# Reordering a gated-linear-attention output stage by tile shape, and its gate matmul as two row tiles

## The reference, cut to what matters

```python
gate_logit = (glr @ p['gla_w_gate_up'] + p['gla_b_gate'])      # rank 16 -> 128 per head
log_a = log_sigmoid(gate_logit) / GLA_TAU
bcum = cumsum(log_a within a chunk)
q_t, k_t, k_end = qc * exp(bcum), kc * exp(-bcum), kc * exp(b_last - bcum)
A = where(causal, q_t @ k_t^T, 0)
o_intra = A @ vc
dS = k_end^T @ vc
S_next = exp(b_last) * S + dS
o_inter = q_t @ S_start
o = rms_norm(o_intra + o_inter) * silu(gog)
```

## Time and profile before

| | before |
|---|---|
| median of 3 runs | 1530.92 us |
| lowest, highest | 1530.88, 1531.73 us |
| the profiled execution's own time | 1532.95 us |
| its span | 1531.2 us |
| granted TensorE clock, mean | 0.998 |
| PE matmul busy | 98% of the span |
| DVE, ACT busy | 45%, 40% |

### The profile page before, as it was taken

The page is one execution under the profiler, slowest core; times in us unless marked ns, Lnnn a source line. Parts: engine busy times, 40 slices in busy tenths (PEclk is TensorE's granted clock), DMA queues, the critical chain, the costliest instruction groups (busy, mean ns, idle before and its releaser), DMA issues.

```text
span 1531.2 us, 25468 instructions
## 1 busy us (share of the span) xinstructions
PE 1499.9 (98%) x9798; PEld 1393.1 (91%) x9798; DVE 691.3 (45%) x1190; ACT 606.9 (40%) x1100; POOL 10.8 (1%) x25
## 2 busy tenths in 40 slices
PE   6999999999999999999999999999999999999998
PEld 6989999999999999998988989998998998998986
DVE  5555555542358774233544453245432323323335
ACT  5333333322147772134554642134541441531532
POOL 1000000000000000000000000000100000000000
PEclk9999999999999999999999999999999999999999
DMA  5556445432312222232432422253122222222222
GB/s 160 151 133 163 126 125 156 108 86 70 82 50 80 74 69 73 83 100 56 115 106 63 113 82 73 76 186 97 42 74 77 71 81 83 69 82 68 78 89 82
DMA packets 224962, 143.58 MB, mean 94 GB/s; under 512 B 7655, under 2 KB 211112, under 8 KB 224893
## 3 DMA queue, kind: packets, MB, share of 16 engines
q1 hardware_dynamic: 224900, 142.72, 32.8%
HBM read 129.86 MB, written 12.84 MB: 93 GB/s over the span
## 4 chain that ended last, share of the span: by engine, by line
PE 85%; DVE 6%; ACT 4%; issue 3%; DMA 1%; SPq 1%; DVEq 0%; ACTq 0%
PE psum L591 55%; PE psum L1007 18%; PE psum L748 1%; PE psum L776 1%; DMA w_raw<-in_w_in_dram 1%; PE psum L639 1%; PE psum L931 1%; DVE arena L1938 1%; ACT arena L1392 1%; PE psum L602 1%; DVE arena L1994 1%; PE psum L759 1%; PE psum L974 1%; PE psum L972 1%; PE psum L708 1%
## 5 line engine op out<-in xcount | busy, mean ns | idle before, releaser
L591 PE MATMUL psum<-XH,w_hi 128*128 128x320 f32 x1872 | 589.9, 315 | 3.8 <-ACT arena L1382 1.8
L591 PE MATMUL psum<-XH,w_lo 128*128 128x320 f32 x1872 | 579.7, 310 | 0.0
L591 PE MATMUL psum<-XL,w_hi 128*128 128x320 f32 x1872 | 579.6, 310 | 0.0
L1662 DVE TENSOR_TENSOR w_lo<-w_raw,w_hi 128x1024 fp32r<-128x1024 f32 x177 | 216.5, 1223 | 355.4 <-ACT w_hi L1194 354.7
L591 PEld LDWEIGHTS psum<-XH,w_hi 128*128 128x128 f32 x1872 | 352.3, 188 | 16.9 <-issue 8.9
L591 PEld LDWEIGHTS psum<-XL,w_hi 128*128 128x128 f32 x1872 | 352.4, 188 | 0.7
L591 PEld LDWEIGHTS psum<-XH,w_lo 128*128 128x128 f32 x1872 | 352.0, 188 | 0.0
L1194 ACT CAST w_hi<-w_raw 128x1024 fp32r<-128x1024 f32 x177 | 185.2, 1047 | 306.3 <-PE psum L1007 154.1
L1007 PE MATMUL psum<-w_hi,YL 128*128 128x512 f32 x280 | 109.1, 390 | 0.0
L1007 PE MATMUL psum<-w_hi,YH 128*128 128x512 f32 x280 | 109.1, 390 | 0.0
L1007 PE MATMUL psum<-w_lo,YH 128*128 128x512 f32 x280 | 109.1, 390 | 0.0
(11 more groups left out here) (276 smaller groups left out, 1713.8 us busy)
## 6 DMA issues: line engine op xcount, KB each, us to landing
w_raw<-in_w_in_dram SPq DMA_DIRECT2D x88, 512.0 KB, 3.9
w_raw<-in_w_up_dram SPq DMA_DIRECT2D x32, 512.0 KB, 4.1
w_raw<-in_w_down_dram SPq DMA_DIRECT2D x32, 512.0 KB, 3.5
w_raw<-in_w_branch_dram SPq DMA_DIRECT2D x24, 512.0 KB, 3.8
arena<-in_cache_fox_k_dram SPq DMA_DIRECT2D x8, 1024.0 KB, 5.8
arena<-in_cache_fox_v_dram SPq DMA_DIRECT2D x8, 1024.0 KB, 7.9
out_dram<-arena SPq DMA_DIRECT2D x16, 256.0 KB, 2.4
arena<-in_state_gla_dram SPq DMA_DIRECT2D x4, 1024.0 KB, 5.6
```

The costliest lines, as they stand in the source:

```text
L591: mm = pe.matmul(Z[h][:, 0:HT], w[s][:, k, :], x[:, k, h * HT:(h + 1) * HT], start=(k == 0 and i == 0), stop=(k == KT - 1 and i == 2))
L1662: dve.tensor_tensor(dst, src, h.bitcast(F32), ALU.subtract).then_inc(w_lo, 1)
```

## The change

The outputs get a bank each, GO = banks 6, 7, 4, 5, 2, and PE does first all five full matmuls, then the eight 64-column ones, then the eight 32-column ones; go_done is signalled as each tile's last matmul ends. The waits for go_read between outputs go; one wait for all five readouts now stands before the sample states, since they reuse banks 2, 4 and 5. The turned outputs go to banks 6, 7 and 4 (O_TURN), and only the last tile's two transposes wait for a state signal, the seventh, which frees bank 4. The gate's input glr is laid out as two tiles of token halves, one in rows 0 to 15 and one in rows 32 to 47, GU is loaded twice, and each gate matmul uses its own 32-row tile of the array; gu_in then counts 32 a head.

```diff
--- before.py
+++ after.py
@@ -156,6 +156,7 @@
             return ctx.enter_context(nc.semaphore(name))
 
 
+        GRP = 2 * TS_
         psum = ctx.enter_context(nc.psum_tensor("psum", [P, 8, 512], F32))
         bank = [psum[:, i, :] for i in range(8)]
         Z = bank[0:2]
@@ -183,7 +184,7 @@
         col = sb("col", [P, KT, NR])
         lru_c4 = sb("lru_c4", [P, 2, LRU_N])
         bcol = sb("b_fox_col", [FOX_HEADS, 1])
-        glr = sb("glr", [GLA_RANK, T])
+        glr = sb("glr", [2 * GRP, HT])
         cn = sb("c_nat", [P, NT, FOX_HEADS])
         small = sb("small", [P, 12, 8])
         lfn = sb("logf_nat", [P, NT, FOX_HEADS])
@@ -313,7 +314,6 @@
 
             return v[:, TP:T].rearrange("p (b t) -> p b t", t=TS_)
 
-        GRP = 2 * TS_
         NGRP = NB // 2
 
         def parted(v):
@@ -326,6 +326,12 @@
 
         def grp(g):
             return slice(g * GRP, (g + 1) * GRP)
+
+        def rank_rows(q):
+            return slice(q * GRP, q * GRP + GLA_RANK)
+
+        GO = [bank[i] for i in (6, 7, 4, 5, 2)]
+        O_TURN = [bank[i] for i in (6, 7, 4)]
 
         def tok(t):
             return slice(t * P, (t + 1) * P)
@@ -509,7 +515,8 @@
                 if not first:
                     load(b, s, w_in_v[:, :, c(cgk, P)])
                     sp.wait_ge(gg_mm, h.v)
-                sp.dma_start(GU[0:GLA_RANK, :], gla_up[0][:, c(0, P)]).then_inc(gu_in, 16)
+                for q in range(2):
+                    sp.dma_start(GU[rank_rows(q), :], gla_up[0][:, c(0, P)]).then_inc(gu_in, 16)
                 load(b + 1, 1 - s, w_in_v[:, :, c(cgv, GLA_DV)])
                 load(b + 2, s, w_in_v[:, :, c(cgv, GLA_DV, P)])
                 if not first:
@@ -878,10 +885,11 @@
             def turn_o(h):
 
                 pe.wait_ge(go_ready, (h + 1).v)
-                pe.wait_ge(ds_read, (h * 8 + 8).v)
                 for t in range(NT):
+                    if t == NT - 1:
+                        pe.wait_ge(ds_read, (h * 8 + 7).v)
                     for e in range(2):
-                        mm = pe.transpose(TBK[t // 2][:, (2 * (t % 2) + e) * P:(2 * (t % 2) + e + 1) * P],
+                        mm = pe.transpose(O_TURN[t // 2][:, (2 * (t % 2) + e) * P:(2 * (t % 2) + e + 1) * P],
                                           OS[:, t, e * P:(e + 1) * P], idf[:, :])
                 mm.then_inc(gt_turned, 1)
 
@@ -894,14 +902,14 @@
 
                     if some:
                         turn_o(h + -1)
-                    pe.wait_ge(gu_in, (h * 16 + 16).v)
+                    pe.wait_ge(gu_in, (h * 32 + 32).v)
                     if some:
                         pe.wait_ge(ds_read, (h * 8).v)
                         pe.wait_ge(at_ready, (h * 2).v)
                     else:
                         pe.wait_ge(last_sb, 1)
                     for q in range(2):
-                        mm = pe.matmul(SBK[q][:, 0:HT], GU[0:GLA_RANK, :], glr[:, q * HT:(q + 1) * HT], start=True, stop=True)
+                        mm = pe.matmul(SBK[q][:, 0:HT], GU[rank_rows(q), :], glr[rank_rows(q), :], start=True, stop=True)
                     mm.then_inc(gg_mm, 1)
 
                 def turn_ke():
@@ -945,6 +953,7 @@
                         rows = grp(i // 2)
                         return KEM[rows, i % 2, :], VN[rows, NTP, :]
                     pe.wait_ge(kem_ready, (h + 1).v)
+                    pe.wait_ge(go_read, (h * 5 + 5).v)
                     pe.wait_ge(ds_read, (h * 8 + 4).v)
                     pe.wait_ge(at_ready, (h * 2 + 2).v)
                     states(DS_SAMPLE, part)
@@ -960,30 +969,24 @@
                         if t >= 3:
                             mm.then_inc(at_done, 1)
 
-                def out(t):
-
-                    O = (TBK[2], OBK)[t % 2]
-                    if t == NTP:
-                        pe.wait_ge(s0_in, (h * 16 + 16).v)
-                    pe.wait_ge(at_ready, (h * 2 + (1 if t < NTP else 2)).v)
-                    if t >= 2:
-                        pe.wait_ge(go_read, (h * 5 + (t - 1)).v)
-                    if t < NTP:
-                        pe.matmul(O[:, 0:GLA_DV], AT[:, t, :], VN[:, t, :], start=True, stop=False)
+                def out_tiles():
+
+                    for t in range(NT):
+                        if t in (0, NTP):
+                            pe.wait_ge(at_ready, (h * 2 + (1 if t < NTP else 2)).v)
+                        pe.matmul(GO[t][:, 0:GLA_DV], AT[:, t, :], VN[:, t, :], start=True, stop=False)
+                    for t in range(NTP):
                         for c in range(2):
-                            mm = pe.matmul(O[c * GLA_CH:(c + 1) * GLA_CH, 0:GLA_DV], QG[:, t * P + c * GLA_CH:t * P + (c + 1) * GLA_CH],
-                                           SA[:, 2 * t + c, :], start=False, stop=True)
-                    else:
-                        pe.matmul(O[:, 0:GLA_DV], AT[:, t, :], VN[:, t, :], start=True, stop=False)
-                        for c in range(2):
-                            for g in range(NGRP):
-                                mm = pe.matmul(O[grp(g), 0:GLA_DV], QGB[:, c, grp(g)], S0[:, 2 * g + c, :], start=False,
-                                               stop=(c == 1))
+                            mm = pe.matmul(GO[t][c * GLA_CH:(c + 1) * GLA_CH, 0:GLA_DV],
+                                           QG[:, t * P + c * GLA_CH:t * P + (c + 1) * GLA_CH], SA[:, 2 * t + c, :],
+                                           start=False, stop=True)
+                        mm.then_inc(go_done, 1)
+                    pe.wait_ge(s0_in, (h * 16 + 16).v)
+                    for c in range(2):
+                        for g in range(NGRP):
+                            mm = pe.matmul(GO[NTP][grp(g), 0:GLA_DV], QGB[:, c, grp(g)], S0[:, 2 * g + c, :], start=False,
+                                           stop=(c == 1))
                     mm.then_inc(go_done, 1)
-
-                def out_tiles():
-                    for t in range(NT):
-                        out(t)
 
                 block(b, s, XH, XL, (gate, None))
                 block(b + 1, 1 - s, XH, XL)
@@ -1228,7 +1231,7 @@
 
                 act.wait_ge(z_done[h], 1)
                 step(act.activation(fz[0:FOX_HEADS, h * HT:(h + 1) * HT], Z[h][0:FOX_HEADS, 0:HT], ACT.Identity, bias=bcol[:, :]))
-                act.copy(glr[:, h * HT:(h + 1) * HT], Z[h][32:32 + GLA_RANK, 0:HT]).then_inc(z_free[h], 1)
+                act.copy(glr[rank_rows(h), :], Z[h][32:32 + GLA_RANK, 0:HT]).then_inc(z_free[h], 1)
 
             def first_q(h, O):
 
@@ -1446,7 +1449,7 @@
                 for j in range(3):
                     n = 2 if j < 2 else 1
                     for e in range(2):
-                        src = TBK[j].rearrange("p (t e d) -> p t e d", e=2, d=P)[:, 0:n, e, :]
+                        src = O_TURN[j].rearrange("p (t e d) -> p t e d", e=2, d=P)[:, 0:n, e, :]
                         dst = OT[:, e, 2 * j * P:(2 * j + n) * P].rearrange("p (t d) -> p t d", d=P)
                         ins_ = act.activation(dst, src, ACT.Copy, scale=col[:, e, R_GN:R_GN + 1])
                     ins_.then_inc(gt_copied, 1)
@@ -1519,7 +1522,7 @@
                         act.activation(half(SG[:, e, :], q), Z[q][:, 0:HT], ACT.Tanh, scale=0.5).then_inc(sg_tanh, 1)
                         if (e, q) == (1, 0):
                             for t in range(NT):
-                                O = (TBK[2], OBK)[t % 2]
+                                O = GO[t]
                                 act.wait_ge(go_done, (h * 5 + (t + 1)).v)
                                 step(act.copy(OS[:, t, :], O[:, 0:GLA_DV]))
                                 act.activation(E2[:, 0:GLA_DV], O[:, 0:GLA_DV], ACT.Square,
```

More of the change, by code:

```diff
@@ L961, in scores @@
                             mm.then_inc(at_done, 1)
-                def out(t):
-                    O = (TBK[2], OBK)[t % 2]
-                    if t == NTP:
-                        pe.wait_ge(s0_in, (h * 16 + 16).v)
-                    pe.wait_ge(at_ready, (h * 2 + (1 if t < NTP else 2)).v)
-                    if t >= 2:
-                        pe.wait_ge(go_read, (h * 5 + (t - 1)).v)
-                    if t < NTP:
-                        pe.matmul(O[:, 0:GLA_DV], AT[:, t, :], VN[:, t, :], start=True, stop=False)
-                        for c in range(2):
-                            mm = pe.matmul(O[c * GLA_CH:(c + 1) * GLA_CH, 0:GLA_DV], QG[:, t * P + c * GLA_CH:t * P + (c + 1) * GLA_CH],
-                                           SA[:, 2 * t + c, :], start=False, stop=True)
-                    else:
-                        pe.matmul(O[:, 0:GLA_DV], AT[:, t, :], VN[:, t, :], start=True, stop=False)
-                        for c in range(2):
-                            for g in range(NGRP):
-                                mm = pe.matmul(O[grp(g), 0:GLA_DV], QGB[:, c, grp(g)], S0[:, 2 * g + c, :], start=False,
-                                               stop=(c == 1))
-                    mm.then_inc(go_done, 1)
```

## The result

The changed kernel takes 1521.53 us, median of 6 runs (1520.51 to 1522.85), against 1530.83 of the kernel before (6 runs too): ratio 0.9941, 95% interval [0.9931, 0.9951], 9.3 us less, by the interval 7.5 to 10.6.

What follows compares the result with a forecast made beforehand. The prediction took TensorE, busy 98% of the span, as the bound. It summed 0.53 (head 0's gate) + 5.04 (three head-to-head stretches) + 1.61 (after head 3) = 7.2 us, so 1530.92 - 7.2 = 1523.7 us, range 1522.2 to 1527.0.

Steps and rivals of the forecast that it cites:

- term 1: Output stage, outputs grouped by shape: takes 5.09 us instead of 6.37, PE leaves 1.28 us earlier in each of four heads.
- Term 2: Gate in two row tiles running side by side: 0.73 us instead of 1.27, saving 0.53 per head.
- rival A: Gate: the two row tiles do not overlap, 2.1 us of the saving falls away, 1525.9 us; chance 0.11.
- Rival B: Output stage: weight loads show in the 64-column run, losing 1.07 us of term 1's 1.28; 1526.6 us; chance 0.09.
- The readout chain: ACT's readouts after the outputs: first copy later, pace 0.91 us instead of 1.21, DVE's state additions only about 0.1 later.
- d: Shift of the chain from ACT's table load to DVE's eight state additions: about 0.1 us later, 0.2 if hops cost more.
- Head to head: turn_o to next projection: PE waits about 0.5 us at the gate for DVE's additions; 1.68 saved three times, 5.04 us.
- rival C: Gate's wait is hidden, additions come 0.5 us earlier than reckoned, both terms kept whole: 8.2 us, 1522.7; chance 0.04.
- Ends: First and last head: 0.53 us saved at head 0's gate, 1.61 after head 3, where no gate follows.
- Costed at nothing: Second GU load on SP, glr copies, state stores and S0's load: no cost; GU uncovered would cost 0.38 us a head.
- D: Readouts keep the old pace of 1.21 us, chain ends at 727.2: 3.6 us saved, 1527.3; chance 0.06.
- E: Slower: readouts start only after the whole output stage and their chain delays the head's end: +7.6 us, 1538.5; chance 0.04.

Runs made afterwards that it cites:

- e3: Changed kernel with its five banks and no waits for readouts, but outputs again tile by tile (full, 64 columns, full, 64 columns): 1526.84 us, ratio 0.9974.
- e2: Kernel before with only the gate as two row tiles (two GU loads): 1529.11 us, ratio 0.9988.
- e1: Changed kernel with the gate put back to one 16-row tile and one GU load: 1524.94 us, ratio 0.9960.
- e5: Changed kernel with one unused 256-column square on ACT between the fifth readout and the root: 1521.85 us, ratio 0.9945.
- e12: Kernel before, unchanged, a third time, for one more profile of the stretch ahead of the first gate: 1530.29 us for the one execution.
- e10: Changed kernel once more, unchanged, on the same chip: 1521.89 us, ratio 0.9943.
- e11: Changed kernel with DVE's k_end product first, then the low part of the fourth block's weight, the k_t product last: 1521.26 us, ratio 0.9936.

## Why the prediction was wrong

- **Pace, output stage, term 1: right.** 5.13 us against 5.09, 1.24 less than before in each head (1.28 forecast). That the 0.35 of a period is not the wait for ACT is shown by e3.
- **Term 2: right.** 0.53 a head alone (e2) and on top (e1); the 16-row tiles overlap, rival A is out. **Rival B** is out too: sixteen 64-column instructions take 1.87 us with the way to the next shape, where 4 x 0.427 + 0.15 is 1.86. The Trainium skill's rule ("TensorEngine Tiling (Array Packing)", Restrictions) that column tiling disables Fast Weight Load brings no cost to this run: the loads of 0.13 us stay hidden though it comes back to each tile. What Fast Weight Load itself would change, no run here shows.
- **The readout chain: here it failed.** The step reads "some 0.91 with the hop to the next". I summed the copy to the end of the accumulator read and added a hop. The next copy starts while the accumulator is still being read (720.17 + 0.20 against 720.26): the pace is 0.77. Five readouts take 3.98 from the first copy to the table load instead of 4.55; the first copy came 2.95 into the stage, as forecast (2.92). So the table load stands 6.93 us after the stage's start instead of 7.41 before, and d is -0.5, not +0.1. The additions even end 0.62 earlier, 14.43 after the stage's start (730.97) instead of 15.05. The other 0.14 is a second thing that the chain had wrong: it hung the additions on the silu alone, but before they started only 1.24 after PE's sample states had begun (728.67 to 729.91, and 725.87 to 727.11 in e3). The first of these states' signals stands in the trace at 729.81, near the silu's end (729.85), in the changed kernel at 726.52, before the silu begins (726.85). There they bind no more: the first addition starts 1.87 after the states and 0.40 after the start of the silu. Timeline of the kernel before, then of e3:

```profile
729.91 3.72 DVE L1994 SCALAR_TENSOR_TENSOR arena<-arena,psum 128x256 f32<-128x256 f32 x8
...
725.87 1.15 PE L939 MATMUL psum<-arena 32*128 32x256 f32 x16
...
727.11 3.72 DVE L1997 SCALAR_TENSOR_TENSOR arena<-arena,psum 128x256 f32<-128x256 f32 x8
```

- **Head to head: wrong by this alone.** With the additions 0.62 earlier they are over when PE comes to the gate. The half microsecond that was to be lost three times is kept: 55.87 from gate to gate, 0.4 below the forecast, 1.2 us in three heads. That is the gap between 7.2 and the stage's 8.4, and it is rival C ("the additions come 0.5 us earlier than reckoned", 8.2), to which I gave 0.04. Its chance was too low because I tied it to the table loads, which stayed, and did not ask how sure the 0.91 was. e5 shows how near the two cases are: 0.44 us more on ACT and a wait of 0.29 at the gate is back.
- **Ends: right.** turn_o's 0.33 went in all four heads (0.30 to 0.38 each, 1.33 in all). The stage's 8.41 is 4 x (1.24 + 0.53 + 0.33) = 8.40.
- **Nothing outside the stage: wrong by 0.4 us.** Ahead of the stage it holds, by e12 and e10. Behind it the end of the program is 0.4 shorter. The stage alone would put the time at 1530.83 - 8.4 = 1522.4, inside the range; with the end it is 1522.0, just outside. The rest from 8.8 to the 9.3 of the medians lies within their interval (from 7.5) and is not explained.
- **Slips in the rivals' sums**, of no weight for the forecast. C takes one 0.33 off that the main sum rightly keeps: its terms give 8.56, 1522.4 us. D leaves out that the last head's last two transposes would wait 0.9 for the sixth addition, which makes it 2.7 and not 3.6. By the same count the loss outweighs the gain from d = 2.0 on, not 2.5.
- **Costed at nothing: right inside the stage.** PE has no wait for GU, S0 or the scores in the changed kernel, and the wait of 0.21 before the fourth block stayed as it was.
- D and E are out: the first copy starts 2.95 into the stage, PE does not wait before the sample states.

## What to carry to other kernels

Group small matmuls by tile shape before asking anything else: each pair of shape changes cost 0.35 us here, nearly as much as one fp32 matmul of 256 columns (0.43), and more banks alone (e3) did not bring it back. When a chain moves behind a bound engine, price its pace from two of its rows that follow without a wait; if the trace of before has none, keep both ends in the range: 0.14 us a link, over four links, turned a lost half microsecond per head into a kept one. Ask of every instruction in the chain what else it waits for, since another engine that comes earlier may let it go earlier too. Compare a stage by its own start and end when executions drift by as much as the change brings, and look at the end of the program as well.

## What was not expected of the hardware

ACT starts a PSUM copy 0.77 us after the one before it although the first copy, square and accumulator read together span 0.88: the copy overlaps the read of the accumulator (720.17 + 0.20 against 720.26), while the table load waits for its end (723.25 + 0.19 against 723.47).

Ahead of the stage, at about 76 us, PE waits for DVE, after ACT had waited 6 to 7 us for the DMA of one weight (6.41 in the first profile of the kernel before, up to 72.80). In the two profiles of the kernel before that were 2.0 and 3.5 us above their medians this wait was 2.11 and 2.96 us, and behind it the granted clock averaged 0.90 to 0.93 over 70 to 90 us: half speed (0.50, the lower of its two levels) for some 3 us, 128x320 matmuls of 0.47 us instead of 0.31. In e12, e10 and the changed kernel the wait was 2.05, 2.18 and 1.66 us and the clock stayed at 1.00; in e11 it was 2.40, longer than the 2.11, and the clock stayed up too. The length of the wait alone doesn't tell the two cases apart, and what does stays open. What is shown is that the same program runs with the fall and without it, in a place that the change does not touch. None of the eleven profiles of kernels with the change, whole or in part, has the fall; whether that is more than chance is not known.
